# When a weight panel's two parts fall due: a second, earlier step beside the first part of the panel two back

## The reference, cut to what matters

```python
# block 1
mod = silu(c) @ w_ada + b_ada                       # six vectors of 1024
h = rms_norm(x, norm1_w) * (1 + scale1) + shift1
proj = h @ w_in                                     # dn q,k,v,z,alpha,beta; mla q,ckv,kr; two gates
o_a = gated_delta_rule(q_a, k_a, v_a, g_a, beta_a)  # chunks of 64, a state passed from chunk to chunk
y_a = (rms_norm(o_a, dn_norm_w) * silu(dn_z)) @ w_out_dn
o_b = mla_attention(...)                            # w_uk, w_uv, norms of q and k, rope, softmax
x = x + gate1 * ((sigmoid(gate_dn) * y_a + sigmoid(gate_mla) * (o_b @ w_out_mla)) @ w_o)
x = x + gate2 * (conv_gelu(up_a) * up_v) @ ffn_w_down
# block 2
proj = rmsnorm(h, norm1_g) @ w_in                   # rwkv, attention, index, two gates
y_a = rwkv7_mix(...)                                # chunks of 64 here too, a state passed on
y_b = dsa_attention(...)                            # index scores, the 128 largest of a row, softmax
h = h + (g_a * (y_a @ w_o_rwkv) + g_b * (y_b @ w_o_att)) @ w_out
h = h + (silu(z_gate) * z_up) @ w_ffn_out
return rmsnorm(h, normf_g)
```

## Time and profile before

| | |
|---|---|
| median of 3 runs | 2142.48 us (2141.2 to 2143.66) |
| profiled execution, its own time | 2142.85 us |
| its span | 2141.0 us (1.85 us lie around it) |
| TensorE busy | 95% of the span |
| VectorE, ScalarE, GpSimd busy | 42%, 38%, 46% |
| granted TensorE clock, mean | 0.977 of full |

### The profile page before, as it was taken

One profiled execution on the slowest core, in us unless ns is written; L12 is line 12 of the kernel. 1 busy time (PEld: TensorE's weight loads), 2 busy tenths in 40 slices (PEclk: granted clock), 3 DMA queues, 4 the chain that ended last, 5 costly groups with the idle time before them and its releaser, 6 DMA issues.

```text
span 2141.0 us, 26269 instructions
## 1 busy us (share of the span) xinstructions
PE 2031.1 (95%) x10166; PEld 1639.2 (77%) x10166; DVE 909.1 (42%) x1508; ACT 804.8 (38%) x1057; POOL 982.3 (46%) x766
## 2 busy tenths in 40 slices
PE   6997899999999999999999888989999999999997
PEld 3785896875778887888888576966887788888886
DVE  1679554766433044232200587457944452111101
ACT  3565224346554224222222543343225743222221
POOL 3636613644313464655555373013443265565652
PEclk9998999999999999999999899999999999999999
DMA  6311104721112332222233211011222222222222
GB/s 274 99 60 59 40 1 200 277 79 40 47 53 79 113 123 79 95 92 92 97 117 115 92 60 60 2 50 40 99 79 79 81 98 99 99 99 99 98 99 79
DMA packets 29482, 194.87 MB, mean 91 GB/s; under 512 B 5040, under 2 KB 7216, under 8 KB 8752
## 3 DMA queue, kind: packets, MB, share of 16 engines
q1 hardware_dynamic: 29360, 193.19, 24.8%
HBM read 188.99 MB, written 4.19 MB: 90 GB/s over the span
## 4 chain that ended last, share of the span: by engine, by line
PE 81%; DVE 12%; ACT 3%; DMA 2%; POOL 1%; issue 1%; SPq 0%; ACTq 0%; DVEq 0%; POOLq 0%
PE ps L411 22%; PE ps L412 21%; PE ps L413 21%; PE ps L471 2%; DVE ar L2391 1%; DVE sm L2390 1%; DMA ar<-ada_dram 1%; DVE ar L1844 1%; POOL WL L2476 1%; PE ps L827 1%; PE ps L840 1%; PE ps L501 1%; DVE ar L1870 1%; PE ps L895 1%; DVE ar L1944 1%
## 5 line engine op out<-in xcount | busy, mean ns | idle before, releaser
L2476 POOL TENSOR_TENSOR WL<-raw,WH 128x512 fp32r<-128x512 f32 x588 | 774.1, 1317 | 951.5 <-ACT WH L1278 915.3
L411 PE MATMUL ps<-hH,WH 128*128 128x512 f32 x1648 | 662.1, 402 | 27.9 <-POOL WL L2476 6.6
L413 PE MATMUL ps<-hH,WL 128*128 128x512 f32 x1648 | 648.4, 393 | 0.0
L412 PE MATMUL ps<-arR,WH 128*128 128x512 f32 x1392 | 542.5, 390 | 0.0
L1278 ACT CAST WH<-raw 128x2048 fp32r<-128x2048 f32 x147 | 280.8, 1911 | 503.5 <-DMA raw<-panels_dram 501.9
L411 PEld LDWEIGHTS ps<-hH,WH 128*128 128x128 f32 x1648 | 313.9, 190 | 110.3 <-issue 36.1
L413 PEld LDWEIGHTS ps<-hH,WL 128*128 128x128 f32 x1648 | 313.7, 190 | 67.3
L412 PE MATMUL ps<-xL,WH 128*128 128x512 f32 x848 | 336.6, 397 | 0.0
L412 PEld LDWEIGHTS ps<-arR,WH 128*128 128x128 f32 x1392 | 262.0, 188 | 54.3 <-issue 0.2
L411 PE MATMUL ps<-arR,WH 128*128 128x512 f32 x592 | 230.6, 390 | 1.4 <-DVE ar L1927 1.4
L413 PE MATMUL ps<-arR,WL 128*128 128x512 f32 x592 | 230.3, 389 | 0.0
(11 more groups left out here) (376 smaller groups left out, 2230.2 us busy)
## 6 DMA issues: line engine op xcount, KB each, us to landing
raw<-panels_dram SPq DMA_DIRECT2D x145, 1024.0 KB, 4.8
ar<-ada_dram SPq DMA_DIRECT2D x12, 2048.0 KB, 12.0
xT<-xT_dram SPq DMA_DIRECT2D x2, 2048.0 KB, 9.4
out_dram<-xT SPq DMA_DIRECT2D x8, 512.0 KB, 2.6
xT<-out_dram SPq DMA_DIRECT2D x1, 2048.0 KB, 10.8
wide<-wide_dram SPq DMA_DIRECT2D x1, 1024.0 KB, 6.7
raw<-panels_dram SPq DMA_DIRECT2D x1, 992.0 KB, 5.7
raw<-panels_dram SPq DMA_DIRECT2D x1, 960.0 KB, 6.0
```

Of the source, the lines that this page charges most:

```text
L411: mm(out, lhs[0], rhs[0], start=first, stop=False)
L412: mm(out, lhs[0], rhs[1], start=False, stop=False)
L413: return mm(out, lhs[1], rhs[0], start=False, stop=final)
L2476: ins = tt(WL[:, n % SLOTS, c], raw[:, n % SLOTS, c], WH[:, n % SLOTS, c].bitcast(F32), ALU.subtract)
```

## The change

`panel_due(n)` decides in front of which wait the parts of panel n are put. Before, that was the first part of panel n - 2. Now it is the lesser of that and six steps past the release of the ring place that panel n takes over.

```diff
 SLOTS = 3
+LANDED = 6
...
         def panel_due(n):
 
-            return 0 if n < 2 else panel_part[0] if n == 2 else panel_part[n - SLOTS + 1]
+            return 0 if n < 2 else panel_part[0] if n == 2 else min(panel_part[n - SLOTS + 1], panel_release[n - SLOTS] + LANDED)
```

## The result

| | before | after |
|---|---|---|
| median of 4 runs each | 2142.12 us (2141.2 to 2143.66) | 2160.89 us (2159.83 to 2164.11) |
| span of the profiled execution | 2141.0 us | 2158.0 us |
| granted clock, mean | 0.977 | 0.974 |

After to before is 1.0083, 95% interval 1.0068 to 1.0098: the kernel is 18.8 us slower by the medians, 17.0 us by the two spans. The forecast was 2157.8 us, 15.3 us slower. The two profiled executions begin alike: up to the sums of qss (490 us) each matmul starts within 0.2 us of its time before. Lines from `LANDED` on count one more than before.

The account below looks back on a forecast made before the run. The chain of waits was taken as four fifths TensorE, most of the rest VectorE; 3.5 + 2.3 + 2.2 + 5.4 - 9.7 + 1.4 + 10.2 (clock) = +15.3 us, giving 2157.8 us, range 2147 to 2163.

Parts of the forecast that it names:

- 14, 15, 26, 99: 0: At the new places of panels 14, 15, 26 and 99: the moves cost and gain nothing, 0 us.
- Sums of kss, 3.5 and 2.7 for the clock: Panels 27 and 28: stop at kss 2 goes, nearly 6 us at kss 3 comes; +3.5 us, half speed +2.7.
- 33 and 109, 2.3 and 2.2 and twice 2.7: Both attentions' ends: ScalarE waits for the panel's load, values 15 starts later; +2.3 and +2.2 us, half speed 2.7 each.
- 90 early, +5.4: Before nv: panel 90's quarters hold up GpSimd's clearing, TensorE's stop grows from 1.84 to 7.2 us; +5.4 us.
- third rival: Before nv: VectorE's inversion covers the late clearing, the 5.4 and 2.1 go; 2150.3 us, chance 0.05.
- Its clock, +2.1: Behind the 7.2 us stop before nv: half speed, of which only the next 4 us feed the chain; +2.1 us.
- fifth rival: Dearer: one clock fall lasting twice as long, or VectorE slowed in more places; above 2163 us, chance 0.07.
- 90 at ai, -9.7: At ai, where panel 90 is used: the 6.61 us stop and 3.1 us of half speed go; -9.7 us.
- 93, +1.4: At the index scores: panel 93's quarters beside VectorE's first index sums for about 3 us slow them; +1.4 us.
- first rival: At the new stops: the clock does not follow, wholly or in part; 2147.6 or 2152.4 us, chance 0.18.
- second rival: Loads, copies and quarters slip into idle time, only the gain at ai is left; 2132.8 us, chance 0.03.
- The fourth: Next to nothing: TensorE's dense stretches behind the stops take them back; 2141.7 us, chance 0.05.

Follow-up runs that it names:

- the kernel with 90 alone: Only panel 90 falls due early (step 482), against the kernel before: 2147.99 us, +4.8 us, ratio 1.0016.
- kernels with only the clearing late: Panel 90 due at 521 and GpSimd's clearing 5.8, 2.3 or 1.2 us later, against the kernel before: 2147.74, 2146.62, 2136.79 us.
- the kernel with 93 alone: Only panel 93 falls due early (step 594), against the kernel before: 2144.44 us, +1.4 us, ratio 1.0010.

## Why the prediction was right, and where its sizes were off

The direction, the places and the number held; the sum was 3.5 us short of the medians and 1.7 of the spans. Single parts measured alone add up to 4.8 + 5.0 + 7.2 + 1.4 = 18.4 us against 18.8 for the whole (by the ratios 16.3 against 17.8), so what follows part by part accounts for the whole.

That the number came so near is in part luck. Held against the table of places, the terms for the sums of kss and for 33 and 109 were too dear by 1.3, 0.9 and 1.3 us, and 2.0 us were given back that no term has: 5.5 us too much. The clock behind nv was too cheap by 1.4, 93 by 0.7, and the half speed at gmean with the rest (4.6) and the small things (0.4) were in no term: 7.1 us too little. These nearly cancel.

- *14, 15, 26, 99: 0.* Right: 2129.9 against 2129.4 us.
- *Sums of kss, 3.5 and 2.7 for the clock.* TensorE was forecast to go on at 524.8 and did at 524.52. The whole is 5.0 in place of 6.2; the half speed lies partly over the stop itself (521 to 529, work again from 524.52).
- *33 and 109, 2.3 and 2.2 and twice 2.7.* The stops grew by 2.45 and 1.96 us, right. The clock was priced 1.0 us too dear each time: in the changed kernel the half speed lasted 3.4 us behind each, which costs about 1.7, not 2.7. Together 7.2 in place of 9.9. The sizing failed where one row (the stop of 3.57 us in the earlier trace rows, 5.6 us at half speed) was taken for all stops of that size. It does not even hold for its own stop, as shown below.
- *90 early, +5.4.* Right to a tenth: in the kernel with 90 alone the stop before nv is 5.42 us longer. The third rival (VectorE's inversion covers it) falls; kernels with only the clearing late pay the delay in full.
- *Its clock, +2.1.* Mis-sized: nv to the chunk steps takes 23.10 in place of 19.57, +3.5. VectorE's chain waits for these products, so each at half speed counts, the ones behind the first 4 us too.
- *Not in the sum: the half speed at gmean,* 4.7 to 4.9 us, 100 us behind the stop. This is the largest error. The fifth rival had one fall "that lasts twice as long", but none without a stop of its own. It offset the two clock terms that were too large: 90 early was forecast at 5.4 + 2.1 - 9.7 = -2.2 and measures +4.8.
- *90 at ai, -9.7.* Right: 9.72 us in the trace, 10.4 by medians.
- *93, +1.4.* The mechanism was right, its size in the trace 2.1 to 2.2. The quarters end at 1481.04 and the sums begin at 1478.50: in 2.5 us of overlap they lose 1.8, where the rate of the earlier trace rows (0.67 of 1.41) gives 1.2. What was mis-sized is the rate: a sum loses 0.9 us for each quarter that it meets, and it met two. The Trainium skill, page "SBUF — State Buffer", section "Who interferes with whom", says that a VectorE instruction with two SBUF inputs and a GpSimd instruction that reads SBUF exclude each other. The trace agrees: 5.45 beside the quarters, 3.65 without, all of it in the two sums that met a quarter. Only VectorE paid: the four quarters took 5.35 us, against 5.31 in the earlier trace rows.

The first rival, that the clock would not follow the stops, is refused for this kernel: all four new stops have their half speed. But it had more of a chance than its text gave it. "None of that length here speaks against it" held for the one trace at hand. The very stop of 3.57 us in the earlier trace rows comes in all 14 kernels, of which eleven do not differ up to there. Behind it the clock was low for 5.2 to 6.1 us in nine of the traces, for 3.4 us in three and not at all in two (the last five are among the eleven). The reading "after 2.51 us it stayed at 1.00" was true of the kernel before, though its window in the earlier trace rows ends 0.4 us behind the stop; of the eight kernels that have this stop, two were at half speed right behind it. Both show in the kernel with 93 alone, timeline and windows:

```profile
263.13 0.66 PE L617 MATMUL ps<-cm,ar 128*128 128x128 f32 x4 [3.58 <-ACT ar L1412]
...
263.00:270.00 7.00, 6.87 (x62) 6.87 (x63) 2.16 (x4) 3.60 (x7) 3.32 (x3) 1.00 0.02 9
...
516.91 5.40 PE L475 MATMUL ps<-ar,cm 128*128 128x512 f32 x8 [2.52 <-POOL ar L2574]
...
517.00:521.00 4.00, 4.00 (x6) 1.70 (x7) 1.82 (x2) 0.69 (x1) 2.35 (x2) 0.57 0.00 0
```

The second rival (the parts slip into idle time) falls where ScalarE waits for the loads of 33 and 109, 1.29 and 1.49 us. The fourth (dense stretches take the stops back) falls by +5.0 and +7.2 us.

The Trainium skill, page "TensorE: Matmul & The Clock Gate", section "What's actually happening", says that the gate's rhythm does not start with the work. By this the same stop may cost different amounts, and the trace agrees: 0 to 6.1 us of half speed behind the same stop of 3.57 us, and 5.1 or 3.4 us behind that at the MLA's end. It fits the shift too: where the change moved whole stages by 7 to 9 us without touching them, some of their half-speed stretches changed length, and this gave back the 2.0 us of the table. One pair of windows on the same stage shows it, before and after:

```profile
815.00:822.00 7.00, 5.64 (x14) 4.47 (x15) 6.68 (x10) 3.52 (x6) 0.00 (x0) 0.51 0.01 4
```

```profile
825.00:829.00 4.00, 3.63 (x10) 2.90 (x11) 3.82 (x6) 1.69 (x3) 0.00 (x0) 0.57 0.03 6
```

**Open.** Why a stop of 4.17 us or more before nv brings half speed 100 us later at gmean. Four kernels with such a stop have it, ten (the kernel before among them) without it don't, and the place in the span's time is ruled out. That it is carried through the chunk steps by where the clock's changes fall against the work fits all 14 traces and is not shown. Also open is whether panel 28 can be put in front of a square that has slack.

## What to carry to other kernels

A part that is made early must be early against the whole queue in which it is written down: ask what stands behind it, and whether its load has landed and its helper engine is free by then. The panel that was late (90) had to come some 7 us sooner, and a place in an idle stretch 90 us ahead did it at no cost; the rule put it directly in front of the one piece of GpSimd's work that the chain was waiting for. So look for the idle stretch in the trace and give the due step by it. Price a stop of TensorE by the stop and the half speed behind it, up to where its results are next waited for; for a short stop that half speed is a range and not one number (0 to 6.1 us behind the one of 3.57 us).

## What was not expected of the hardware

The cost is not in proportion to the stop. Before nv, 1.17 us more of standing cost 3.2 us by the traces, 2.33 cost 10.4 and 5.83 cost 14.0. A stop of 4.17 us there was followed by a second stretch, 10 us at half speed, a hundred microseconds on.

Nor does the length of a short stop say whether half speed follows. In the 14 traces every one of TensorE's 110 stops of 3.8 us or more between two matmuls has at least 2.8 us of half speed in the 8 us behind it. Of the 58 between 2.5 and 3.7 us, nine have none there, and these are from 2.51 to 3.58 us long; others of 2.6 us have 6. The kernel before has both: none behind 2.51 us, and behind a stop of 2.61 us that ends at 364.86 this window:

```profile
365.00:371.00 6.00, 6.00 (x19) 5.03 (x20) 5.71 (x9) 0.00 (x0) 0.00 (x0) 0.50 0.83 350
```

The kernel before itself ran from 2138.87 to 2152.73 us in 29 runs on one chip. Its granted clock went from 0.980 to 0.972 over these, so changes of a few microseconds needed a dozen runs on either side here. The traces tell where the time goes, but each is one execution, and half-speed stretches that differ between two of them can be chance.
